# Moving the expert search of five heads into the phase before, and turning gate rows out of a repeated column

## The reference

```python
mod = c_act @ ada_w[l] + ada_b[l]
sh_m, sc_m, g_m, sh_f, sc_f, g_f = jnp.split(mod, 6, axis=-1)
h = _rmsnorm(x, norm_mix_g[l]) * (1.0 + sc_m) + sh_m
...            # one projection, three kinds of heads, one output projection: mix
x = x + g_m * mix
h = _rmsnorm(x, norm_ffn_g[l]) * (1.0 + sc_f) + sh_f
x = x + g_f * peer_ffn(h, ...)
```

```python
u = jnp.take(u_tab, eidx, axis=0)
act = jnp.einsum('thkd,td->thk', u, hc)
coef = gate * gelu(act)
return jnp.einsum('thk,thkd->td', coef, jnp.take(v_tab, eidx, axis=0))
```

## The kernel before

| segments | tick | what |
|---|---|---|
| 0 to 2 | 1 | norm, first turn |
| 9, 10, 11, 12, 13 | 6, 7, 8, 8, 9 | VectorE's long part of the recurrence's set-up |
| 33 to 36 | 24 to 27 | levels and attention |
| 46, 47 / 48 | 38 / 39 | gate row of the mixing part |
| 57 to 72 | 49 to 58 | queries and scores |
| 61 to 68 | 51 to 56 | search for heads 0 and 1 |
| 69, 70 / 71, 72 / 73 | 56, 57 / 58 / 59 | (TensorE and ScalarE: queries, scores) |
| 74, 75 / 76, 77, 78 | 60 / 61 | gate row of the channel part |

## Time and profile before

### The profile page before, as it was taken

How to read it: one execution, slowest core, us unless ns; L and a number is a source line. 1 busy time by engine, 2 the same in 40 slices (tenths; PEclk the granted TensorE clock), 3 DMA queues, 4 the chain that set the end, 5 groups by cost and what they waited for, 6 DMA issues and landing times.

```text
span 1901.2 us, 20926 instructions
## 1 busy us (share of the span) xinstructions
PE 1616.6 (85%) x6868; PEld 1006.0 (53%) x6868; DVE 1394.7 (73%) x3315; ACT 673.4 (35%) x1640; POOL 515.2 (27%) x564
## 2 busy tenths in 40 slices
PE   1767678898999998898999998898999997887776
PEld 1656665554665655564665655554665652332222
DVE  5866598997856758998765748988765759985554
ACT  1313114334732334335632235325632233331112
POOL 2000013222233232222233232222232233343331
PEclk9889788998999999998999999999999998999999
DMA  9982688997799999998999999998899999999996
GB/s 393 422 346 101 242 353 348 367 421 286 283 399 421 422 420 395 363 422 313 321 403 421 421 421 399 370 402 293 287 403 421 421 415 401 416 407 421 421 421 256
DMA packets 96989, 706.08 MB, mean 371 GB/s; under 512 B 10992, under 2 KB 11504, under 8 KB 13296
## 3 DMA queue, kind: packets, MB, share of 16 engines
q0 software_dynamic: 80640, 587.24, 77.1%
q1 hardware_dynamic: 16240, 117.50, 15.1%
HBM read 703.64 MB, written 1.05 MB: 371 GB/s over the span
## 4 chain that ended last, share of the span: by engine, by line
PE 49%; DVE 28%; DMA 16%; ACT 3%; issue 3%; POOL 0%; DVEq 0%; ACTq 0%; POOLq 0%
PE psum L772 26%; DMA ringmem<-in_peer_uv_dram,eidx 11%; DVE ringmem L1435 9%; PE psum L648 5%; PE psum L412 4%; DMA W<-in_w_groups_dram 3%; PE psum L635 2%; DMA ringmem<-in_ada_pairs_dram 2%; PE psum L520 1%; PE psum L508 1%; DVE ringmem L1079 1%; PE psum L518 1%; PE psum L415 1%; DVE coef L1448 1%; ACT diag L1050 1%
## 5 line engine op out<-in xcount | busy, mean ns | idle before, releaser
L772 PE MATMUL psum<-ringmem,diag 128*128 128x512 f32 x2048 | 978.4, 624 | 132.3 <-ACT diag L1050 132.0
L379 POOL DMA_INDIRECT ringmem<-in_peer_uv_dram,eidx x512 | 489.5, 956 | 1131.5 <-PE psum L772 1079.7
L1435 DVE SCALAR_TENSOR_TENSOR ringmem<-ringmem,psum 128x1024 f32<-128x1024 f32 x512 | 612.5, 1220 | 195.3 <-DMA ringmem<-in_peer_uv_dram,eidx 180.1
L772 PEld LDWEIGHTS psum<-ringmem,diag 128*128 128x128 f32 x2048 | 389.1, 199 | 608.1 <-issue 409.1
L1050 ACT ACTIVATE diag<-K,coef 128x128 f32<-128x128 f32 x512 | 176.4, 393 | 225.8 <-DVE coef L1448 225.6
L412 PE MATMUL psum<-hT,W 128*128 128x128 f32 x1344 | 172.3, 287 | 40.9 <-DMA W<-in_w_groups_dram 19.1
L412 PEld LDWEIGHTS psum<-hT,W 128*128 128x128 f32 x1344 | 169.2, 203 | 64.9 <-issue 38.0
L1042 ACT ACTIVATE coef<-dots 128x2 f32<-128x2 f32 x256 | 51.8, 202 | 408.6 <-DVE ringmem L1435 407.7
L1079 DVE SCALAR_TENSOR_TENSOR ringmem<-ringmem,diag 128x1024 f32<-128x1024 f32 x96 | 115.3, 1223 | 20.9 <-DMA ringmem<-in_ada_pairs_dram 18.8
L648 PEld LDWEIGHTS psum<-hT,W 128*128 128x128 f32 x1024 | 123.2, 197 | 12.8 <-issue 7.2
L648 PE MATMUL psum<-hT,W 128*128 128x128 f32 x1024 | 126.0, 281 | 3.1 <-ACT hT L821 3.0
(11 more groups left out here) (243 smaller groups left out, 1629.7 us busy)
## 6 DMA issues: line engine op xcount, KB each, us to landing
ringmem<-in_ada_pairs_dram POOLq DMA_DIRECT2D x48, 1024.0 KB, 19.0
W<-in_w_pieces_dram SPq DMA_DIRECT2D x48, 1024.0 KB, 9.2
W<-in_w_groups_dram SPq DMA_DIRECT2D x24, 1536.0 KB, 11.3
W<-in_w_groups_dram SPq DMA_DIRECT2D x12, 1024.0 KB, 9.6
ringmem<-in_peer_uv_dram,eidx POOLq DMA_INDIRECT x512, 11.7
W<-in_w_groups_dram SPq DMA_DIRECT2D x4, 1040.0 KB, 9.2
attn<-in_subkeys_t_dram SPq DMA_DIRECT2D x4, 1024.0 KB, 9.5
K<-in_consts_dram SPq DMA_DIRECT2D x1, 1546.0 KB, 18.1
```

Of the source, the lines that this page charges most:

```text
L379: nc.gpsimd.indirect_dma_start(slot(k), None, rows, bass.IndirectOffsetOnAxis(ap=eidx[:, ph % 2, m:m + 1], axis=0)).then_inc(row_landed[q ...
L772: mm = nc.tensor.matmul(acc[:, q], diag[:, k % DIAGS, :], slot(k)[:, D:][:, q], start=(k % SEL == 0), stop=(k % SEL == SEL - 1), skip_grou ...
L1435: ins = v.scalar_tensor_tensor(out=u, in0=u, scalar=1.0, in1=hrep, op0=ALU.mult, op1=ALU.mult, accum_out=dots[:, j:j + 1])
```

## The change

1. For the phases 1 to 3 five heads instead of two are searched in the phase before: segments 61 to 78 of `mixing(i)` do 18 parts, one in a segment, and segment 78 adds parts 2 and 3 of head 4.
2. A table `find_ticks` gives the ticks of what is left. In phases 1 to 3 heads 5, 6 and 7 are searched in ticks 16 to 27. In phase 0 heads 2 to 4 are searched in ticks 1 to 12 and heads 5 to 7 in ticks 16 to 27.
3. `gate_exp` follows: a tick after each head's part 3, or in segments 65, 69, 73, 77 and 78.
4. A gate row is made by TensorE transposes of a column of `MC` that is read 128 times; `gate_diag` is gone, with its semaphore. The second copy of the mixing gate moves from segment 48 to 47. For the channel gate both halves come in segment 75, in banks 6 and 7, with both copies in ScalarE's segment 75 (at the very end: segment 76).

```diff
+def find_ticks(ph):
+    out = [[] for _ in range(TICKS)]
+    for n in range(12):
+        if ph == 0:
+            out[1 + n].append((2 + n // 4, n % 4))
+        out[16 + n].append((5 + n // 4, n % 4))
+    return out
...
@@ TensorE
-                            gate_row(g_at(i, 0), gdiag[0], bank[4], ("u_sb", at("u_sb", i, 1)))
+                            gate_row(g_at(i, 0), l, G_M, 0, bank[4], ("u_sb", at("u_sb", i, 1)))
...
-                            gate_row(g_at(i, 2), gdiag[1], bank[6], ("q_sb", at("q_sb", i, 7)))
-                        elif i and seg == 76:
-                            gate_row(g_at(i, 3), gdiag[1], bank[6], ("g_sb", g_at(i, 3)))
+                            for half in range(2):
+                                gate_row(g_at(i, 2 + half), (i - 1) // NT, G_F, half, bank[6 + half],
+                                         ("q_sb", at("q_sb", i, 7 + half)))
...
-                    pe.wait_ge(s["g_diag"], nth + 1)
+                    pe.wait_ge(s["mod_ready"], 3 if l else 2)
                     pe.wait_ge(s[bank_free[0]], bank_free[1])
                     for j in range(4):
-                        mm = nc.tensor.matmul(dst[:, j * P:(j + 1) * P], ones[:], src[:, j, :], start=True, stop=True)
-                    mm.then_inc(s["g_out"], 1)
+                        k = 4 * half + j
+                        tr = nc.tensor.transpose(dst[:, j * P:(j + 1) * P],
+                                                 MC[:, l, section, k:k + 1].broadcast_to([P, P]), ident)
+                    tr.then_inc(s["g_out"], 1)
...
@@ ScalarE
                         elif seg == 46:
-                            if i == 0:
-                                act.wait_ge(s["mod_ready"], 2)
-                            gate_diag(l, G_M, 0, gdiag[0])
+                            gate_copy(g_at(i, 0), 0, bank[4][:, :])
                         elif seg == 47:
-                            gate_copy(g_at(i, 0), 0, bank[4][:, :])
-                            gate_diag(l, G_M, 1, gdiag[0])
-                        elif seg == 48:
                             gate_copy(g_at(i, 1), 1, bank[4][:, :])
...
-                        if seg in (65, 69):
-                            gate_exp(i, (seg - 65) // 4)
-                        if i and 75 <= seg <= 77:
-                            if seg > 75:
-                                gate_copy(g_at(i, seg - 74), seg - 76, bank[6][:, :])
-                            if seg < 77:
-                                gate_diag((i - 1) // NT, G_F, seg - 75, gdiag[1])
+                        if seg in ((65, 69, 73, 77, 78) if i else (65, 69)):
+                            gate_exp(i, (seg - 62) // 4)
+                        if i and seg == 75:
+                            for half in range(2):
+                                gate_copy(g_at(i, 2 + half), half, bank[6 + half][:, :])
...
                         activate(n)
-                        if m % 4 == 0 and 2 <= 1 + m // 4 < PH:
-                            gate_exp(ph, 1 + m // 4)
+                        for h, part in FIND[ph][m - 1] if m else []:
+                            if part == 3:
+                                gate_exp(ph, h)
...
@@ VectorE
-                        elif 61 <= seg <= 68:
+                        elif 61 <= seg <= (78 if i else 68):
                             retrieve(i, (seg - 61) // 4, (seg - 61) % 4)
+                            if seg == 78:
+                                retrieve(i, 4, 2)
+                                retrieve(i, 4, 3)
...
-                        if m < 4 * (PH - 2):
-                            retrieve(ph, 2 + m // 4, m % 4)
+                        for h, part in FIND[ph][m]:
+                            retrieve(ph, h, part)
                         beside.upto(PACE[m])
```

More of the change, by code:

```diff
@@ L151, in trunk @@
     PACE, LEAD = pace(), lead_pace()
+    FIND = [find_ticks(ph) for ph in range(PHASES)]
     with ExitStack() as ctx:
@@ L274, in trunk @@
         crow = diag[:].rearrange("p a c -> p (a c)")
-        gdiag = (hT[:, 0:4, :], hm[:, 0:512].rearrange("p (a c) -> p a c", a=4))
         def slot(k):
@@ L738, in mixing, with gate_row @@
                         if i and seg == 75:
-                            gate_row(g_at(i, 2), gdiag[1], bank[6], ("q_sb", at("q_sb", i, 7)))
-                        elif i and seg == 76:
-                            gate_row(g_at(i, 3), gdiag[1], bank[6], ("g_sb", g_at(i, 3)))
-                def gate_row(nth, src, dst, bank_free):
-                    pe.wait_ge(s["g_diag"], nth + 1)
+                            for half in range(2):
+                                gate_row(g_at(i, 2 + half), (i - 1) // NT, G_F, half, bank[6 + half],
+                                         ("q_sb", at("q_sb", i, 7 + half)))
+                def gate_row(nth, l, section, half, dst, bank_free):
+                    pe.wait_ge(s["mod_ready"], 3 if l else 2)
                     pe.wait_ge(s[bank_free[0]], bank_free[1])
                     for j in range(4):
-                        mm = nc.tensor.matmul(dst[:, j * P:(j + 1) * P], ones[:], src[:, j, :], start=True, stop=True)
-                    mm.then_inc(s["g_out"], 1)
+                        k = 4 * half + j
+                        tr = nc.tensor.transpose(dst[:, j * P:(j + 1) * P],
+                                                 MC[:, l, section, k:k + 1].broadcast_to([P, P]), ident)
+                    tr.then_inc(s["g_out"], 1)
                 def last_gate():
[L752 to L755, removed]
+                    yield 75
+                    for half in range(2):
+                        gate_row(g_at(PHASES, half), DEPTH - 1, G_F, half, bank[6 + half],
+                                 ("q_sb", at("q_sb", PHASES, 0)))
                 def place_h(ph):
@@ L791, in gate_exp @@
                     nc.scalar.activation(e, e, exp, accum_out=gsum[:, i % 2, h:h + 1]).then_inc(s["gate_exp"], 1)
[L793 to L797, removed]
                 def gate_copy(nth, half, src):
@@ L1031, in ending @@
                     squares_last(0)
[L1032 to L1037, removed]
+                    yield 76
+                    for half in range(2):
+                        gate_copy(g_at(PHASES, half), half, bank[6 + half][:, :])
                 def activate(n):
```

4 lines of the change are left out of this document (2 added, 2 removed).

## The result

The changed kernel takes **1942.97 us** (median of 6 runs, 1941.11 to 1947.44); the kernel before took 1899.47 us on the same chip (6 runs). The ratio is **1.0233**, 95% interval 1.0212 to 1.0253: slower, and 26 us above the forecast of 1917, outside its range. The profiled execution took 1944.58 us, its span is 1942.8 us against 1901.2.

The account below looks back on a forecast made before the run. VectorE bounds early ticks, TensorE and DMA ticks 12 to 15, DMA the phase ends, the gather phase 3. Terms -16 - 3 + 10.5 + 20.6 + 4 - 0.4 = +15.7 on 1903.0; forecast 1917 us, range 1893 to 1932.

Parts of the forecast that it names:

- Step 1: Ticks 0 to 15 of phases 1 and 2: removed search parts let TensorE recover waits, -8 us each, bounds 4 and 10.
- Step 2: Phase 0: tick 0 is freed and part 3 of head 4 slides past tick 11, -3 us, bounds -4 and 0.
- Step 3: Ticks 24 to 27 of phases 0 to 2: four added search parts make `weigh` late, +3.5 us each, bounds 1 and 9.7.
- Step 4, borders 0 to 1 and 1 to 2: Ticks 56 to 61: 13.8 us of search in tick 61 makes `weigh(63)` 10.3 us late at each border, +20.6 us.
- Step 4, border 2 to 3: Rows in flight cover most of TensorE's standing and phase 3 catches up: +4 us, bounds 0 and 10.
- Step 5: Gate rows by transposes: +0.7 us in tick 38 of three phases, -1.8 at the end; together -0.4, clock effect nothing.
- Rival (d): The clock falls behind the turns, 3.1 us at each of eight gate rows: +25 on the sum, 1942 us; chance 0.03.
- The end: After the last `coefficients`, the sum could start at 1889.5 instead of 1891.33 us: -1.8 us.
- Rival (b): Late `weigh`s at the border cost nothing while rows are in flight, early ticks reach 421 GB/s: 1890 us; chance 0.14.
- Rival (a): It cancels: ticks 24 to 27 cost 1 us each phase, phase starts gain the full 10: 1903 us; chance 0.26.
- rival (c): Ticks 24 to 27 cost the whole 9.7 us and the clock falls at each border: 1948, halfway 1932; chance 0.07.
- The point of decision: Tick 12: whether TensorE reaches its place there despite a start 10 us later, which would favour Rival (b).

Follow-up runs that it names:

- gates_only: Changed kernel's gate rows (transposes, second copy early) with the search as in the kernel before: 1906.19 us, ratio 1.0030 to the kernel before.
- search_only: Kernel before with the change's search schedule and `gate_exp`, gate rows still by diagonals: 1934.19 us, ratio 1.0174 to the kernel before.
- heads_12_23: Changed kernel with heads 5 to 7 searched in ticks 12 to 23 and phase 0's search as in the kernel before: 1924.22 us, ratio 1.0125.
- last_border: Changed kernel, but phase 3 alone searches its head 4 in its own ticks 0 to 3 instead of in tick 61 before: 1933.36 us, ratio 1.0185.
- diag_early_copy: Kernel before with only the second copy of the mixing gate moved from segment 48 to 47: 1901.74 us, ratio 1.0004.
- gates_matmul: gates_only with the transposes written as plain matmuls of the same two operands, early copy kept: 1898.93 us, ratio 0.9991 to the kernel before.
- head4_12_15: Changed kernel with head 4 of phases 1 to 3 searched in ticks 12 to 15 of its own phase instead of tick 61: 1906.00 us, ratio 1.0020.
- four_heads_gap: Kernel before with heads 0 to 3 searched in the phase before, head 4 in ticks 0 to 3, heads 5 to 7 in 12 to 23: 1886.14 us, ratio 0.9920.

## Why the prediction was wrong, step by step

The sign, the mechanism of the tick with head 4 and the largest term were right. The sum was 26 us short. By the ledger the misses are +12.0 at the gate rows (4.1 in front, 7.9 in ticks 28 to 40), +8.5 at the last border, +6.3 in ticks 24 to 27, +3.2 at the first two borders, +2.3 in phase 0 and +0.4 at the end; against them stand -4.8 from tick 63 to tick 24 and -2.1 in ticks 40 to 56. The gate rows' share looks larger there than it is: gates_only is 5.2 us slower as a whole, search_only 33.2, where the sum had -0.4 and +16.1.

- **Step 1** (ticks 0 to 15 of phases 1 and 2, forecast -8 each): right. Ticks 2 to 12 give 8.9 and 8.4 us back, ticks 6 to 11 of phase 1 run at 423 GB/s, and its `weigh(7)` waits for nothing.
- **Step 2** (phase 0, -3): it gave nothing. From tick 0 to tick 12 the lateness goes from 3.5 to 3.7 us, in search_only from -3.9 to -3.5. The same parts stand one tick later, and the wait only moves: `weigh(7)` and `weigh(8)` of phase 0 waited 1.59 and 5.20 us, now `weigh(8)` alone waits 7.04. The -0.7 of the ledger comes behind tick 12, where gates_only, with the search as before, moves by 3.7 us too (3.2 to -0.5).
- **Step 3** (ticks 24 to 27, +3.5 each): mis-sized, +5.3, +5.1 and +6.4. I reckoned `coefficients` late and `weigh` waiting for them, and took TensorE as full up to there. The wait came earlier, at TensorE's attention pieces, whose inputs ScalarE and VectorE make later too (2.20 + 0.84 us), and behind the first of them stands half clock (from 923.76 to 928.44 the pieces of tick 26 take 4.7 us, where the same pieces of tick 25 take 3.0). heads_12_23 shows that the four ticks and nothing else are the cause: 0.0 there.
- **Step 4, borders 0 to 1 and 1 to 2** (+10.3 each): +10.7 and +13.1. The chain of four ticks of phase 1 was right to 0.3 us: 9.25, 4.38, 7.59 and 16.57 us, for 9.2, 4.4, 7.6 and 16.3 worked out; `weigh(61)` starts 13.6 us later than its place (34.4 less 20.8). The second border has the half clock that stood in the bounds, 9.81 instead of 7.13 us for two `weigh`s.
- **Step 4, border 2 to 3** (+4, bounds 0 and 10): **this step failed**. "The rows in flight cover most of the standing", I wrote, and that phase 3 catches up. TensorE did catch up in part; by tick 12 it was back from 47.0 to 37.4. But it was the wrong engine to ask. The gather sets phase 3's end, and a slot comes free only when a `weigh` ends: 13 us without one are 13 us without a new row to fetch, 12.8 us of idle DMA by the share. last_border puts the border at 9.6 us by the medians and 9.2 by the traces: the mechanism stood in the text, priced at less than half.
- **Step 5, the gate rows** (-0.4 together): **failed**, +9.9 in ticks 28 to 40 and +3.5 in front (where kernels with an unchanged front differ by as much), less what comes back after; as a whole +5.2 by gates_only. The turns' own time was right: 0.6 us a half at full clock, 1.04 for eight. I priced the clock at nothing from a projection that ran at 0.13 a record behind eight turns. That row has one run of turns in the middle of matmuls. The mixing gates stand among waits of about a microsecond, and there the clock fell. The second copy, at +0.7, was undersized too: it costs 1.5 us a phase in diag_early_copy. Rival (d) had the mechanism, at 3.1 us for each of eight gate rows; what the clock costs is nearer to 2 us at each mixing gate (2.4 to 3.4 in gates_only against 1.2 in gates_matmul), an amount in front that the spread hides, and nothing that I can see at the channel gates. Its time, 1942, is within 1 us of the measured one by luck: the gate rows alone make 5 us, not 25. I gave it 0.03 on one row against a stated rule.
- **The end** (-1.8): right, -1.7.

Rival (b), the faster side, said that the late tick costs nothing while rows are in flight, and that the early ticks reach full DMA rate. Its second half came true in ticks 6 to 11 and not in ticks 0 to 5 (423 and 348 GB/s), its first did not: head4_12_15 keeps the gain of 10 us and is 37 us faster without the late tick. Rival (a) fell with ticks 24 to 27 and with the last border. Of the mechanisms, rival (c), "it hurts more", came nearest: the clock fell at each border, though of the first two it cost about 3 us at one only, and ticks 24 to 27 cost 5.6 us on average where it had 9.7; what it lacked was tick 38.

The point of decision I gave, tick 12, could not decide. TensorE was 11.8 us late at tick 56 of phase 0 and 11.8 us late at tick 12 of phase 1: it did reach its place there, as (b) asked. But a border that costs 10.7 us before a gain of 10.7 looks the same as a free border before no gain. It took a kernel with the gain and without the border, head4_12_15, to tell them apart.

## What to carry to other kernels

Work moved beside other work costs nothing only where each single tick has room. Of the twelve parts moved into the phase before, eight cost little (0.8, 1.4 and 4.6 us at the three borders of four_heads_gap); taking away the four that fell into one tick gave 37 us. Print the load of each tick before the order is fixed, and look at what a late tick keeps from being issued, not only at which engine can catch up: where a ring of buffers feeds a DMA that is the bound, most of its idle time goes to the end (here 8 of 11 us). And judge a transpose by what stands behind it too: it takes half the time of the plain matmul with the same operands, but next to the early copy the plain one was the cheaper (ratio 0.9991 against 1.0030); with the late copy the two were level (0.9991 and 0.9999).

## What the runs showed of the hardware

- A column read 128 times as the stationary operand costs a turn nothing extra: eight in 1.04 us (at 1141.51 in the changed kernel), as the eight of the earlier trace rows; four take 0.60 to 0.65 us at full clock and 1.06 at half clock.
- The same two operands in a plain matmul take eight records and 1.06 us at full clock, and gates_matmul is faster by them than gates_only (ratio 0.9991 instead of 1.0030); the clock stays up in tick 38 of every phase, and the front has 20.5 us of half clock in the window from 184 to 225 us instead of 34.1.
- In gates_only the clock fell near the gate row of the mixing part, where TensorE has two waits of 1.3 us, at 561.0, 984.2 and 1410.9 us. Over all fourteen traces it did so in 16 of 18 phases with turns and the early copy, in 1 of 6 with turns and the late copy, and in none of 18 with neither or with the copy alone or with plain matmuls.
- Where TensorE stood for some 13 us at a border of the changed kernel, half clock lasted 13.7 us in each of the three phases (from 720.0, 1153.5 and 1593.8 us).
